# Two taps per chunk of a depthwise convolution go from VectorE to ScalarE and GpSimd, and VectorE's odd chain of sums ends in PSUM

## The reference, cut to what matters

```python
def conformer_conv(h, w_pw1, b_pw1, w_dw, b_dw, ln_g, ln_b, w_pw2, b_pw2):
    u = h @ w_pw1 + b_pw1
    a, g = jnp.split(u, 2, axis=-1)
    u = a * jax.nn.sigmoid(g)
    u = lax.conv_general_dilated(        # 31 taps, causal, one filter per feature
        u, w_dw[:, None, :].astype(u.dtype),
        window_strides=(1,), padding=[(CONV_WIDTH - 1, 0)],
        dimension_numbers=("NWC", "WIO", "NWC"),
        feature_group_count=D_MODEL) + b_dw
    u = jax.nn.silu(layer_norm(u, ln_g, ln_b))
    return u @ w_pw2 + b_pw2
```

## Time and profile before

| | us |
|---|---|
| median of 3 runs | 1717.82 (1716.06 to 1718.47) |
| the profiled execution, its own time | 1716.66 |
| its span in the trace | 1714.2 |
| TensorE matmuls busy | 1620.7 (95%) |
| VectorE busy | 1279.6 (75%) |
| ScalarE busy | 1007.8 (59%) |
| GpSimd busy | 217.3 (13%) |

### The profile page before, as it was taken

How to read it: one execution, slowest core, us unless ns; L and a number is a source line. 1 busy time by engine, 2 the same in 40 slices (tenths; PEclk the granted TensorE clock), 3 DMA queues, 4 the chain that set the end, 5 groups by cost and what they waited for, 6 DMA issues and landing times.

```text
span 1714.2 us, 26361 instructions
## 1 busy us (share of the span) xinstructions
PE 1620.7 (95%) x10059; PEld 1408.4 (82%) x10059; DVE 1279.6 (75%) x1363; ACT 1007.8 (59%) x1001; POOL 217.3 (13%) x251
## 2 busy tenths in 40 slices
PE   6987899997979799999999999999999998999996
PEld 4766799996668688888888888888888887999996
DVE  4896476657955898898888988988988987444443
ACT  4555554453134677777776876876877774443333
POOL 0760154531930000000000000000000000000000
PEclk9998899997989999999999999999999998999998
DMA  9954286664756699999999999999999996555301
GB/s 297 341 178 143 94 306 205 217 217 148 257 168 218 256 358 370 340 360 378 342 358 372 340 365 360 345 356 353 366 366 344 363 365 241 197 177 192 123 1 37
DMA packets 231201, 463.26 MB, mean 270 GB/s; under 512 B 18255, under 2 KB 57687, under 8 KB 231127
## 3 DMA queue, kind: packets, MB, share of 16 engines
q1 hardware_dynamic: 229591, 461.55, 76.1%
q10 hardware_dynamic: 1536, 0.68, 0.2%
HBM read 461.15 MB, written 1.05 MB: 270 GB/s over the span
## 4 chain that ended last, share of the span: by engine, by line
PE 85%; DVE 5%; POOL 4%; ACT 3%; DMA 1%; issue 1%; SPq 1%; ACTq 0%; DVEq 0%; POOLq 0%
PE bank L1914 16%; PE bank L1917 16%; PE bank L1920 16%; PE bank L2008 14%; PE bank L1570 12%; PE bank L1728 4%; DVE bank L1182 2%; PE bank L1880 1%; PE bank L1655 1%; PE bank L1960 1%; DMA ring<-in_mod_w_dram 1%; PE bank L1560 1%; PE bank L1613 1%; POOL prod L669 1%; POOL prod L665 1%; POOL part L666 1%
## 5 line engine op out<-in xcount | busy, mean ns | idle before, releaser
L1445 DVE TENSOR_TENSOR wlo<-ring,whi 128x2048 fp32r<-128x2048 f32 x294 | 667.3, 2287 | 95.0 <-PE bank L1920 76.6
L949 ACT ACTIVATE whi<-ring 128x2048 fp32r<-128x2048 f32 x294 | 561.2, 1918 | 163.4 <-PE bank L1917 163.3
L1914 PE MATMUL bank<-whi,xe_hi 128*128 128x512 f32 x784 | 306.9, 391 | 5.1 <-ACT whi L949 5.1
L1917 PE MATMUL bank<-whi,xe_lo 128*128 128x512 f32 x784 | 305.9, 390 | 0.0
L1920 PE MATMUL bank<-wlo,xe_hi 128*128 128x512 f32 x784 | 209.6, 389 | 0.0
L1500 DVE TENSOR_TENSOR wlo<-ring,whi 128x2048 fp32r<-128x2048 f32 x42 | 96.2, 2292 | 113.9 <-ACT whi L988 86.3
L1914 PEld LDWEIGHTS bank<-whi,xe_hi 128*128 128x128 f32 x784 | 147.7, 188 | 36.0 <-issue 5.3
L1917 PEld LDWEIGHTS bank<-whi,xe_lo 128*128 128x128 f32 x784 | 147.7, 188 | 30.6
L1920 PEld LDWEIGHTS bank<-wlo,xe_hi 128*128 128x128 f32 x784 | 147.2, 188 | 30.6
L1914 PE MATMUL bank<-whi,hh 128*128 128x512 f32 x392 | 157.3, 401 | 0.0
L1100 DVE TENSOR_TENSOR ring_lo<-ring,ehi 128x2048 fp32r<-128x2048 f32 x45 | 106.7, 2371 | 63.4 <-ACT ehi L715 63.3
(11 more groups left out here) (366 smaller groups left out, 2532.2 us busy)
## 6 DMA issues: line engine op xcount, KB each, us to landing
ring<-in_moe_w_gate_dram SPq DMA_DIRECT2D x112, 1024.0 KB, 7.2
ring<-in_moe_w_up_dram SPq DMA_DIRECT2D x112, 1024.0 KB, 7.2
ring<-in_moe_w_down_dram SPq DMA_DIRECT2D x112, 1024.0 KB, 6.9
ring<-in_mod_w_dram SPq DMA_DIRECT2D x24, 2048.0 KB, 9.9
ring<-in_ffn_w_gate_dram SPq DMA_DIRECT2D x11, 1024.0 KB, 6.6
ring<-in_ffn_w_up_dram SPq DMA_DIRECT2D x11, 1024.0 KB, 9.0
ring<-in_ffn_w_down_dram SPq DMA_DIRECT2D x11, 1024.0 KB, 5.1
ring<-in_conv_w_pw_dram SPq DMA_DIRECT2D x8, 1024.0 KB, 12.2
```

The lines of the kernel that those rows point to most:

```text
L949: act.activation(whi[:, n % HI_SLOTS, :], ring[:, s * HW:(s + 1) * HW], ACT.Copy).then_inc(hi_ready, 1)
L1445: v.tensor_tensor(wlo[:, n % LO_SLOTS, :], ring[:, s * HW:(s + 1) * HW], whi[:, n % HI_SLOTS, :].bitcast(F32), ALU.subtract).then_inc(lo_r ...
L1914: mm(o[:, :], xh, hi[:, w:w + 512], start=first, stop=False)
L1917: ins = mm(o[:, :], xl, hi[:, w:w + 512], start=False, stop=False)
```

## The change

```diff
-PE_TAPS, POOL_TAPS = 2, 8
+PE_TAPS, POOL_TAPS = 2, 10
...
-                even, odd = conv[:, n, :], tmp[:, n % 2, T:2 * T]
-                sums_at = psum[7][:, 0:T], psum[7][:, T:2 * T]
+                even, odd = conv[:, n, :], psum[7][:, T:2 * T]
+                sums_at = psum[7][:, 0:T], odd
                 for k in range(DVE_FROM, TAPS):
                     a = sums_at[(k - DVE_FROM) % 2]
-                    o = (even, odd)[(k - DVE_FROM) % 2] if k >= TAPS - 2 else a
+                    o = even if k == TAPS - 1 else a
```

## The result

The changed kernel takes 1726.66 us (median of 6 runs, 1725.09 to 1732.94) against 1716.41 us for the kernel before in the same comparison (6 runs): a ratio of 1.0059 with a 95% interval of 1.0048 to 1.0071. It is 10.2 us slower. The prediction said 1728, slower.

A forecast was written before the change was run, and what follows sets the result against it. VectorE bounds the kernel before; after the change GpSimd's chain of adds and other work does, then TensorE's late product. 8.5 + 1.75 = 10.3 us takes 1716.66 to 1727.0, about 1728 against the median; range 1722.5 to 1732.

The forecast's parts named there:

- What bounds the kernel: In the eight chunks VectorE sets the pace, 10.11 us a chunk; GpSimd has 1.8 us of slack in a quiet one.
- What VectorE saves: Per chunk, two multiply-adds go, 0.78 us, and L1189 and L1191 always cost 0.42 us each.
- Chunks 0, 1 and 2: Next gatings at 57.9, 71.0 and 84.9 us; VectorE waits 3.7 us in chunk 1 and 4.6 in chunk 2.
- Chunk 3: Without other work on GpSimd, its adds end at 94.2 us and the next gating comes at 95.0.
- Chunks 4 and 5: GpSimd's state-space products, then block builds, delay its adds; next gatings at 107.2 and 120.5 us, the latter 7.2 us behind.
- Chunk 6: TensorE's late, slow product (8.59 us) puts chunk 7's gating at 131.9 us, 8.5 us behind.
- rival of GpSimd alone: Only GpSimd's adds count: 7.2 + 1.75 = 9.0 us, 1726.7, or 1725 if ScalarE's copies find room; chance 22%.
- The tail: Behind chunk 7's gating, the sums for the mean wait for ScalarE's copies, so L1195 comes 1.75 us later.
- The sum: At L1195, 8.5 + 1.75 = 10.3 us later, with nothing behind it absorbing the delay.
- rival of the intended gain: VectorE stays the bound in the eight chunks, together -10.7 us, 1707 us; chance 5%.
- hidden further down: A later stage that waits for weights takes up the delay, 1718 to 1720 us; chance 5%.
- One slip: In the chunks, ScalarE's product k + 1 was said to need only add k - 3, so ScalarE keeps up.

The follow-up runs named there:

- light GpSimd with ten taps: The change with GpSimd's state-space work between the chunks cut to a token; stage only, chunk 7's gating 71.03 us behind chunk 0's.
- PSUM end alone: The kernel before with the odd chain ending in PSUM, GpSimd keeping eight taps; 1714.35 us, ratio 0.9988.
- kernel with the filled wait: The change with twelve matmuls that nobody reads in TensorE's 5.7 us wait ahead of chunk 4's product; 1727.87 us, ratio 1.0077.
- larger ring: The change with eight buffers for ScalarE's products instead of four; 1724.09 us, ratio 1.0042.
- shorter adds: The change with GpSimd adding only 128 of 256 tokens; stage only, chunk 7's gating 70.23 us behind chunk 0's.
- taps alone: The kernel before with ten taps on GpSimd instead of eight, the odd chain still ending in SBUF; 1729.88 us, ratio 1.0079.

## Why the prediction was right

**What bounds the kernel.** Right as to the slack: ninth add late by 0.7 us in a quiet chunk, as light GpSimd with ten taps shows. Incomplete in "VectorE sets the pace": TensorE has the same pace, 20.34 us for two chunks, which I had not worked out, though rows 1 had it busy for 78.62 of the 87 us.

**What VectorE saves.** Right: the multiply-adds went, L1189 and L1191 never took over 0.43 us, and the PSUM end alone gained 3.15 us in the stage.

**Chunks 0, 1 and 2.** Right within 0.2 us, each with its wait: 3.32 and 4.38 us against 3.7 and 4.6, the rest of chunk 1's having gone into L1187's wait for TensorE.

**Chunk 3.** This step failed: "84.9 + 9.26 = 94.2 for the adds, next gating 95.0". It was 97.53. The adds ended in time, but ScalarE's copy for TensorE stood behind chunk 2's products, which I had followed only for the last chunks; TensorE waited 5.71 us and then ran at 1.2 GHz. The kernel with the filled wait has the same late copy and gates at 94.94, so the clock behind the wait is the whole difference.

**Chunks 4 and 5.** 107.63 and 120.90 against 107.2 and 120.5: the 2.5 us of chunk 3 were nearly absorbed, as GpSimd had been working ahead in the meantime, and its four products took 4.11 us, where the sum has 4.47. In chunk 5 TensorE's taps (119.65 for L1187) and GpSimd's last add (120.07) came at the same time.

**Chunk 6.** This step failed as well: TensorE's late product was to set the gating of chunk 7, at 131.9. VectorE did wait for TensorE (0.47 us, not about 2), but the product of chunk 7 took 7.07 us and not 8.59, GpSimd's ninth add came last (0.31 us of waiting at L1189), and the gating came at 131.01, 10.11 us behind the one before. That is the rival of GpSimd alone, which had 10.07 us for this chunk. I had kept the slow value because TensorE would wait longer before it; it waited 3.27 us before the last transposes ahead of it, and the clock stayed at 1.00.

**The tail.** Mechanism right, size short: 15.07 us and not 14.2, since the last transposes ran at the lower clock (1.94 us instead of 1.11) and ScalarE's copies waited for them. The larger ring brought B back to 12.54.

**The sum.** 10.3 us predicted at L1195, 10.23 measured, and 10.25 in the medians. The errors of chunks 3 to 5, of chunk 6 and of the tail are +0.4, -1.3 and +0.9 us and cancel; that the total is so close is luck, that it is near 10 is not. By place, 7.62 us stand at chunk 7's gating and 2.61 in the tail, where the sum has 8.5 and 1.75. The 1.3 us between 1728 and 1726.66 come from the kernel before, whose median is 1716.41 in this comparison and was 1717.82 in the one that the prediction started from. The **rival of the intended gain** fell twice over: GpSimd's pitch was 0.87 us, and even with shorter adds A was 70.23 us and not 66.3. The **rival of GpSimd alone** (9.0 us) was right for chunk 6 and would have missed chunk 3 and the slower transposes of the tail. **Nothing was hidden further down**, the whole shift arrived at the end. One slip changed nothing: ScalarE's product k + 1 needs add k - 4, not k - 3, as the sum for chunk 6 has it (the tenth needs the fifth).

## What to carry to other kernels

Before work is moved to an engine that looks idle over the whole span, write down when it delivers within one turn of the loop, with all its other work in its order: here it had 1.8 us of slack in a turn, VectorE's saving took 0.78 us of that, and it was given 1.75 us more, with blocks of 4 to 6 us between the turns. Ask also what stands behind the added work on each engine's queue, since an engine that waits for a full ring holds back everything behind it. And check whether a second engine has the same pace as the bound one, which caps the gain whatever is taken off the first.

## What the runs showed of the hardware that I had not expected

TensorE's granted clock after a wait is not told by the length of the wait in these traces. Behind 2.42 us (before) and 2.52 us (eight buffers) the following product took 8.59 and 10.10 us at 0.50 at first; behind 3.27 us (after) it took 7.07 us at 1.00. One and the same execution shows both: with eight buffers the wait of 2.52 us was followed by the slow product, and the next one of about that length was not:

```profile
113.92 0.63 PE L1596 MATMUL bank<-ident,cblk 128*128 128x128 f32 x4 [2.48 <-ACT cT L750]
...
115.25 7.07 PE L1613 MATMUL bank<-yT,ring 128*128 128x256 f32 x32
```

Why is open. Matmuls that nobody reads, put into such a wait, kept the clock for the work right behind them each time: the product took 7.15 instead of 10.05 us, the sums for the mean 3.72 instead of 5.75, the sums of squares 3.69 instead of 6.60.

A block build on GpSimd, which took 1.27 to 1.34 us before and 1.26 to 1.41 with the taps alone, took 1.26 to 1.28 in every kernel in which VectorE's last adds have one SBUF input, and the four products ahead of chunk 4 went from 4.47 to 4.10 or 4.11 us. So the stretch went both ways, though GpSimd's share of it was small.
